# A transformer block and two expert layers on one core: the second rows of pairs 1 to 87 summed on VectorE, one pair behind their dots

## The reference, cut to what matters

```python
def chunk(args):                      # 128 tokens at a time
    xi, ei, gi = args
    hid = jax.nn.gelu(jnp.einsum("td,tkd->tk", xi, u_tab[ei]))   # first row: a dot with the token
    return jnp.einsum("tk,tkd->td", gi * hid, v_tab[ei])         # second row: a weighted sum
...
for l in range(DEPTH_2):
    ...                               # attention, convolution and recurrence: the mixer
    x = x + mixed @ w_out[l]
    h2 = rms_norm(x, norm2_g[l])
    x = x + peer(h2, peer_wq[l], peer_k1[l], peer_k2[l], peer_u[l], peer_v[l])
```

## Time and profile before

| | us |
|---|---|
| median of three runs | 2280.4 (2276.66 to 2283.9) |
| profiled execution, its own time | 2286.74 |
| its span in the trace | 2284.9 |
| TensorE matmul busy | 1832.9 |
| VectorE busy | 1310.2 |
| ScalarE busy | 837.1 |
| GpSimd busy | 589.7 |

### The profile page before, as it was taken

How to read it: one execution, slowest core, us unless ns; L and a number is a source line. 1 busy time by engine, 2 the same in 40 slices (tenths; PEclk the granted TensorE clock), 3 DMA queues, 4 the chain that set the end, 5 groups by cost and what they waited for, 6 DMA issues and landing times.

```text
span 2284.9 us, 21250 instructions
## 1 busy us (share of the span) xinstructions
PE 1832.9 (80%) x7020; PEld 1028.4 (45%) x7020; DVE 1310.2 (57%) x3403; ACT 837.1 (37%) x2144; POOL 589.7 (26%) x516
## 2 busy tenths in 40 slices
PE   7988988866789998789677868866787886777776
PEld 3448755642335855547224535522444642222222
DVE  2324226368624532663997494599477479844444
ACT  1323113133424631552344363243356333533333
POOL 0000000014312111222344233344242344533331
PEclk9979999868899999989888989998898998999999
DMA  9556765449889989969999979999997989999997
GB/s 354 203 196 234 298 233 222 180 160 342 306 333 402 347 310 357 368 249 371 374 410 407 417 297 387 388 407 396 365 399 279 400 346 419 407 420 420 420 420 310
DMA packets 108526, 774.30 MB, mean 339 GB/s; under 512 B 12160, under 2 KB 12416, under 8 KB 16256
## 3 DMA queue, kind: packets, MB, share of 16 engines
q0 software_dynamic: 73728, 536.90, 58.8%
q1 hardware_dynamic: 34688, 236.04, 26.4%
HBM read 771.85 MB, written 1.05 MB: 338 GB/s over the span
## 4 chain that ended last, share of the span: by engine, by line
PE 44%; DMA 25%; DVE 21%; ACT 6%; issue 3%; POOL 1%; SPq 0%; POOLq 0%; ACTq 0%; DVEq 0%
PE psum L458 11%; DMA ring<-in_peer_dram,eidx 10%; PE psum L819 10%; PE psum L472 8%; DMA ring<-in_slabs_dram 7%; PE psum L661 6%; DMA arena<-in_peer_dram,eidx 5%; DVE arena L1758 3%; PE psum L679 3%; DVE ring L1758 2%; DVE x L1769 2%; DMA kv<-in_peer_dram,eidx 2%; DVE kv L1758 2%; PE psum L636 1%; DVE mixs L1613 1%
## 5 line engine op out<-in xcount | busy, mean ns | idle before, releaser
L1818 POOL DMA_INDIRECT arena<-in_peer_dram,eidx x260 | 297.8, 1145 | 1100.4 <-DVE eidx L1737 492.0
L819 PE MATMUL psum<-arena,diag 128*128 128x512 f32 x876 | 460.9, 662 | 128.5 <-ACT diag L1149 95.9
L1758 DVE CUSTOM_DVE_ANT_0 arena<-arena,osb 128x1024 f32<-128x1024 f32 x260 | 316.1, 1221 | 182.3 <-DMA arena<-in_peer_dram,eidx 181.8
L1139 ACT ACTIVATE wexp<-hid 128x1 f32<-128x1 f32 x512 | 103.3, 202 | 751.7 <-DVE hid L1758 748.0
L819 PEld LDWEIGHTS psum<-arena,diag 128*128 128x128 f32 x876 | 170.5, 209 | 378.2 <-ACT diag L1149 194.8
L819 PE MATMUL psum<-ring,diag 128*128 128x512 f32 x456 | 240.5, 654 | 69.6 <-ACT diag L1149 65.2
L458 PE MATMUL psum<-ring,hT 128*128 128x512 f32 x560 | 258.9, 613 | 21.0 <-DMA ring<-in_slabs_dram 14.0
L819 PE MATMUL psum<-kv,diag 128*128 128x512 f32 x412 | 212.2, 646 | 54.7 <-ACT diag L1149 47.0
L1818 POOL DMA_INDIRECT ring<-in_peer_dram,eidx x132 | 155.5, 1178 | 293.9 <-PE psum L819 206.6
L1758 DVE CUSTOM_DVE_ANT_0 ring<-ring,osb 128x1024 f32<-128x1024 f32 x132 | 161.2, 1221 | 81.2 <-DMA ring<-in_peer_dram,eidx 81.1
L1818 POOL DMA_INDIRECT kv<-in_peer_dram,eidx x120 | 136.3, 1136 | 272.8 <-PE psum L819 162.9
(11 more groups left out here) (328 smaller groups left out, 1861.2 us busy)
## 6 DMA issues: line engine op xcount, KB each, us to landing
ring<-in_slabs_dram SPq DMA_DIRECT2D x206, 1024.0 KB, 7.0
ring<-in_slabs_dram SPq DMA_DIRECT2D x8, 768.0 KB
arena<-in_peer_dram,eidx POOLq DMA_INDIRECT x260
ring<-in_slabs_dram SPq DMA_DIRECT2D x8, 512.0 KB, 4.5
ring<-in_peer_dram,eidx POOLq DMA_INDIRECT x132
kk<-in_keys_dram SPq DMA_DIRECT2D x2, 1024.0 KB, 11.1
kv<-in_peer_dram,eidx POOLq DMA_INDIRECT x120
rowg<-in_rows_dram SPq DMA_DIRECT2D x3, 512.0 KB, 14.2
```

The lines of the kernel that those rows point to most:

```text
L819: ins = pe.matmul(bank(b), diags_of(n), pair(slot_of[n])[:, 1024 + 512 * h:1536 + 512 * h], start=(k == 0), stop=(k == 127))
L1139: act.activation(wn, hid[:, 128 * t + k:128 * t + k + 1], ACT.Gelu_apprx_tanh).then_inc(*up("gelu", n))
L1758: v.tensor_tensor_reduce(out=row, in0=row, in1=row_y[t], scale=1.0, scalar=0.0, op0=ALU.mult, op1=ALU.add, accum_out=hid[:, c:c + 1]).then ...
L1818: pool.indirect_dma_start(pair(i), None, tables, bass.IndirectOffsetOnAxis(ap=eidx[:, 128 * t + k:128 * t + k + 1], axis=0)).then_inc(sig. ...
```

## The change

Pairs 1 to 87 are all summed on VectorE (before: 18 of them). When the oldest pair that waits is one for VectorE, it is finished as soon as more than one pair waits, in all tiles. The order between two sums on VectorE is kept by the pair that was summed last instead of by n - 5.

```diff
+ALONE = 88
...
         def on_vector(n):
 
-            return n < 384 and n % 128 not in (0, 127) and n % SHARE == 2
+
+            return n < 384 and n % 128 not in (0, 127) and (n < ALONE or n % SHARE == 2)
...
             def finish_pairs(n):
 
-                while len(late) > n:
+                while late and len(late) > (min(n, 1) if on_vector(late[0]) else n):
                     m = late.pop(0)
                     plan.append(("down", m))
...
                 if on_vector(n):
                     w.wait_ge(*at("weight", n))
-                    if n - SHARE >= 128 * (n // 128):
-                        w.wait_ge(*at("accumulate", n - SHARE))
+                    if last[0] // 128 == n // 128:
+                        w.wait_ge(*at("accumulate", last[0]))
...
-            last = [0]
+            last = [-1]
```

## The result

The changed kernel takes 2304.8 us (median of 4 runs, 2301.6 to 2307.2) against 2281.0 us (4 runs) of the kernel before: a ratio of 1.0105, 95% interval 1.0084 to 1.0125. It is slower by some 24 us, where a gain of 7 was forecast. The profiled execution has a span of 2305.4 us against 2284.9.

A forecast was written before the change was run, and what follows sets the result against it. No engine bounds throughout: VectorE is nearly full beside the routing, then TensorE is busiest with DMA close to full. The terms +21.0 - 33 + 6.4 - 1 = -6.6, say -7 us, gave 2273.5 us, range 2254 to 2295.

The forecast's parts named there:

- A: Stretch beside the routing, 498 to 597 us: 24 more sums on VectorE add 21.0 us; bounds +12 to +28.8.
- B to D, what is removed: B (gates, output), C (feed-forward), D (first half of next mixer): 45 pairs leave TensorE, -33 us.
- Slab-fed pairs: Seventeen pieces (29.2 us) between matmuls that read slabs: half of what is taken off comes back, 14.6 us.
- (L + C) / 2: Period per slab in a ring of two when load L exceeds TensorE's time C: from 9.0 to about 8.2 us.
- The natural test: Where VectorE's own pair fell, TensorE ran 112 records unbroken, then waited 1.57 us for the slab, nearly the whole 1.72.
- Six pieces at other places: Around B1's attention, output and norm and in mixer M01: 18 of 22.0 us come back, some lost to waits.
- B to D, what VectorE adds: 45 more sums on VectorE; five counted on the chain, around B1's norms and in M01: +6.4 us, bounds 0 and 15.
- Rival 3: VectorE becomes the bound in more places, a sum in each mixer hop costing 15 us: net +2, 2282 us; chance 0.17.
- The shorter lag: Everywhere: VectorE's pairs in later tiles finish one pair sooner, -1 us; bounds -8 and +4.
- The rule on queues that take turns: Slab loads: DMA engines alternate between queues packet by packet, so earlier free slots would halve a slab's rate whenever gathers wait.
- Rival 1: Gathers crowd out slabs; no slab-fed pair gives anything once L exceeds 10.9 us: net +14, 2295 us; chance 0.20.
- The sum: Whole kernel: +21.0 - 33 + 6.4 - 1 = -6.6, say -7 us.

The follow-up runs named there:

- run 1: Kernel before with only the shorter lag of VectorE's pairs, every fifth pair still on VectorE: ratio 1.0005.
- run 2: Changed kernel, but only the pairs beside the routing (1 to 31) move to VectorE, the block's pairs stay as before: ratio 1.0065.
- run 3: Changed kernel, but only pairs 32 to 87 (block and mixer) move to VectorE, those beside the routing stay as before: ratio 0.9995.
- run 6: Changed kernel, but only pairs 32 to 69 move to VectorE, those beside routing and mixer as before, short lag: 2269.7 us, ratio 0.9938.
- run 5: Changed kernel with the old lag for all pairs, so VectorE's sums free their slots two pairs later in the block: ratio 1.0132.
- run 4: Changed kernel, with TensorE doing two matmuls of constants wherever pairs 32 to 67 were summed: ratio 1.0124.
- run 7: Kernel before with only half of each weight slab of B1 loaded, TensorE's work unchanged: 2264.2 us, one run.
- run 8: Kernel before with pairs 32 to 87 on VectorE, short lag, and only half of each B1 slab loaded: 2260.5 us, one run.
- run 12: Changed kernel with only pairs 32 to 69 moved, plus matmuls of constants on TensorE in place of each of 32 to 67: 2283.7 us, one run.
- run 11: Changed kernel with only pairs 32 to 87 moved, sums of 70 to 87 covering only 512 of 1024 columns: mixer's first half 89.7 us, one run.

## Why the prediction was wrong

- **A, +21.0 us: right.** Measured +19.8 us, and 19.5 us between runs 1 and 2 (99.6 and 119.1 us). VectorE was busy 117.9 of 119.5 us, and the waits for gathers shrank from 7.8 us to 1.0. Taking the pairs off TensorE gave nothing there, as foreseen.
- **B to D, what is removed, -33 us: this step failed.** In B and C together nothing came back (279.4 to 280.9 us; 277.4 in run 3). Part of that is the new lag's doing: against run 2, which differs from the changed kernel in the pairs 32 to 87 alone, B and C got 7.2 us shorter (288.1 to 280.9), and the best case, run 6 against run 1, gave 12.2 (287.9 to 275.7) of 51.6 us taken off. By the old lag the move gave nothing either (279.4 before, 283.2 in run 5). The step had two terms.
  - *Slab-fed pairs, 14.6 us.* The text put it so: "half of what is taken off comes back as time". It took the load's time L as given, near 9 us, and C, TensorE's time for a slab, as 7.3, which makes a period of 8.2 us. The period was 9.25. C was 7.9 (16.25 and 7.43 us for three slabs), as part of the work ran at the low clock; by (L + C) / 2 the period then asks for an L of 10.6. The pieces of slab loading in the chain of the changed kernel's up projections are

```profile
758.26 11.47 DMA ring<-in_slabs_dram
...
786.42 11.08 DMA ring<-in_slabs_dram
...
814.11 11.31 DMA ring<-in_slabs_dram
```

  in place of 9.87 and 8.29 us. A chain holds the longest loads. Counted over all ten slabs of the up projections from the packets in the traces (from the issue of a slab's second half to its last packet), L was 7.9 us on average before, 9.3 in the changed kernel, and 7.5 in run 4, which differs from the changed kernel only in that TensorE has its work back. So a faster TensorE makes its own loads longer, and L is no constant. The likely way: once TensorE waits, the next load is issued while the last is still under way, and a gather with it, and they share the DMA engines; how much of the growth is overlap and how much gathers was not separated. With 9.3 and 7.9 the rule gives 8.6 us, so it too falls short, by some 0.6 us a slab, which no run explains. It need not always be so: in run 6 the pieces in the middle of C are

```profile
777.64 8.44 DMA ring<-in_slabs_dram
793.95 8.54 DMA ring<-in_slabs_dram
810.38 8.41 DMA ring<-in_slabs_dram
```

  and four slabs from 769.81 to 802.54 us took 8.2 us each, the period forecast. The natural test in the earlier trace rows, a wait of 1.57 us where 1.72 us of work was missing, had shown nine tenths given back, and I read half out of it. Runs 7 and 8 show the cause for C (with half the bytes the move pays 20.2 us), runs 4 and 12 its counterpart (62 us of TensorE's work for 4 and 13 us).
  - *Six pieces at other places, 18 of 22.0 us.* They had in large part covered waits for VectorE, which the text named and put at 4 us. What TensorE waits for around the norms of B1, first before, then changed:

```profile
PE psum L486 <- DVE scr L1487: 3.4, 1, 3.4
PE psum L486 <- DVE scr L1441: 2.7, 1, 2.7
PE psum L486 <- DVE scr L1432: 1.7, 1, 1.7
```

```profile
PE psum L488 <- DVE scr L1489: 8.0, 1, 8.0
PE psum L488 <- DVE scr L1443: 6.1, 1, 6.1
PE psum L488 <- DVE scr L1434: 3.1, 1, 3.1
```

  7.8 us became 17.2, and in the convolution of M01 a wait for VectorE of 12.5 us is new.
- **B to D, what VectorE adds, +6.4 us: too small.** In B and C sums are nearly hidden (1.8% of the chain over 281 us, 5 us, for 2.5 before). In D, 14 pairs moved and the stretch grew by 8.4 us, by 12.5 us against run 2 and by 13.3 us between runs 6 and 3. I had counted five more sums on the chain; in run 3's D the trace shows 13.9 us of them, about eleven at 1.28 us, where run 6 has two. Run 11 bears out their length for about half: 5.3 us came back for 10. Rival 3, a sum in each hop, named this at 15 us and had the size right.
- **The shorter lag, -1 us: right in total within what can be measured** (run 1), but it is a trade and not nothing: +7.8 us in C, -4.4 in D, -6.2 in the second tile. With all 87 pairs on VectorE the traced spans of run 5 and the changed kernel differ by 8.5 us in favour of the shorter lag, while their intervals of the ratio overlap.
- **The rule on queues that take turns** stands where gathers wait all the time, at the start of B and in the down projections of the changed kernel, where a load took 15.85 us. Rival 1, which was built on it, gave 2295 us and ended on the right side by a cause that is only partly its own. Its bound was the right one: with C at 7.3 no slab-fed pair gives anything once L is above 10.7 (the text says 10.9). Its cause, the earlier release of slots, is borne out by run 1 (+7.8 us in C), but not in the changed kernel, where later releases did not shorten the block (run 5).
- **The sum** had the right terms and the wrong size in two: -33 was about 0, +6.4 was +8 to +13. With 0 and +10 it is 21 + 0 + 10 - 1 = +30. The five stretches grew by 28.5 us; the earlier first dot and the tiles behind took 8 off, which leaves the 20.5 of the spans, and the medians differ by 24.

## What to carry to other kernels

Before work is taken off an engine that is 90% busy, ask what its waits would be if it were faster: if it is fed through a ring of two by transfers at a DMA share of 0.88, most of the time taken off turns into waiting, and the load time is no constant in that sum (7.9 us became 9.3, and 7.5 with the work put back). A place where the work is already missing now and then is a good witness, and its measured give-back is to be used as it stands. Compare a change of several parts with a kernel that has all parts but one: the kernel before alone hid that the lag cost C 8 us and the move gave some back. Move work only where the receiving engine is off the path: the same move was worth some 15 us beside the block (ratios 1.0005 and 0.9938 of runs 1 and 6) and cost 20 us beside the routing and 13 us in the mixer. And before half-size loads are taken as a test of supply, ask whether the number of packets fell or only their size.

## What the runs showed of the hardware

- The granted clock fell around TensorE's waits: in the changed kernel 128 records of the up projection took 16.2 us behind waits of 2.81 and 2.86 us, and 64 took 7.43 us behind one of 1.23 us. In run 8, where the slabs came in time, it was 0.98 over the feed-forward without any pair. This agrees with the Trainium skill, "TensorE: Matmul & The Clock Gate", section "What's actually happening", where an idle array is at 1.2 GHz and a busy one at 2.4.
- Beside gathers that are under way, a slab's load gets half of the DMA engines while both move packets of 8 KB. From 855 to 873 us in the changed kernel, with both queues at work throughout, the view is (packets, MB, share)

```profile
q0 software_dynamic: 516, 3.81, 50.7%
q1 hardware_dynamic: 512, 3.79, 50.5%
```

  and the load issued there took 15.85 us. With packets of 4 KB against 8 KB (run 8, above) it was 456 packets to 466, and 32 to 69% of the time. The Trainium skill, "DMA: Bandwidth & Descriptors", section "Queues, rings and completion order", has the engines take turns packet by packet; the trace agrees. Over a few us the split can be far from even: from 794 to 798 us in the changed kernel it was 77 to 23, in favour of the gathers.
